# A hybrid decoder layer in one launch: the norm's feature factors move into the weights on GpSimd, x tiles and gate rows are made further ahead, and the running maxima take one scan

## What is computed

```python
xn = x * rsqrt(mean(x*x, -1) + 1e-6) * norm_gain          # rows factor, then features factor
proj = xn @ w_in                                          # 1024 -> 9*512 + 8
gb, gc, hc, zc, q, k, v, o, zm, ig, fg = split(proj)
y_conv = gb * short_conv(gc * hc) * silu(zc)
lf = log_sigmoid(fg + b_fgate); ig = ig + b_igate         # 4 heads, per token
b = cumsum(lf)                                            # within chunks of 128
m_t = max(b + m_prev, max_{s<=t}(b_t - b_s + ig_s))       # running maximum, carried over chunks
h, c, n, m = mlstm_chunk(q, k, v, ig, lf, c, n, m)        # 4 heads of 128, chunk after chunk
y_m = rms(h) * mh_norm_gain * sigmoid(o) * silu(zm)
y = rmsnorm(x + concat(y_conv, y_m) @ w_out, final_norm_gain)
```

## Time and profile before

| | us |
|---|---|
| median of 3 runs (lowest, highest) | 1136.21 (1135.74, 1137.62) |
| the profiled execution, its own time | 1135.65 |
| its span, first to last instruction | 1133.9 |
| PE busy in the span | 1071.8 (95%) |
| DVE busy | 526.0 (46%) |
| ACT busy | 338.8 (30%) |
| POOL busy | 258.3 (23%) |
| mean granted TensorE clock | 0.983 |

### The profile page before, as it was taken

The page is one execution under the profiler, slowest core; times in us unless marked ns, Lnnn a source line. Parts: engine busy times, 40 slices in busy tenths (PEclk is TensorE's granted clock), DMA queues, the critical chain, the costliest instruction groups (busy, mean ns, idle before and its releaser), DMA issues. The chain is left out here.

```text
span 1133.9 us, 17984 instructions
## 1 busy us (share of the span) xinstructions
PE 1071.8 (95%) x7186; PEld 607.4 (54%) x7186; DVE 526.0 (46%) x1018; ACT 338.8 (30%) x672; POOL 258.3 (23%) x332
## 2 busy tenths in 40 slices
PE   1789989989999999999999999999999999999996
PEld 1646545445566655556566556465656565444442
DVE  5667765655533443445443433544433323334333
ACT  5453333424321323243223232432222222221111
POOL 6101220302020223120213131211121111442322
PEclk9879999999999999999999999999999999999998
DMA  9453150415220031172101213510212053255652
GB/s 268 94 140 72 49 131 24 102 43 159 63 85 7 12 93 61 41 206 81 48 8 49 74 44 112 171 36 20 83 47 89 19 165 142 88 192 209 236 208 84
DMA packets 124311, 109.25 MB, mean 96 GB/s; under 512 B 42392, under 2 KB 109092, under 8 KB 124228
## 3 DMA queue, kind: packets, MB, share of 16 engines
q1 hardware_dynamic: 84160, 66.78, 20.3%
q0 software_dynamic: 7600, 25.03, 6.2%
q10 hardware_dynamic: 32468, 16.30, 5.2%
HBM read 65.95 MB, written 33.41 MB: 88 GB/s over the span
## 5 line engine op out<-in xcount | busy, mean ns | idle before, releaser
L783 PE MATMUL bank<-xTh,Wh 128*128 128x512 f16 (+2 forms) x1304 | 423.3, 344 | 3.7 <-DMA xTl<-to 2.3
L784 PE MATMUL bank<-xTl,Wh 128*128 128x512 f16 (+2 forms) x1304 | 425.9, 343 | 0.0
L785 PE MATMUL bank<-xTh,Wl 128*128 128x512 f16 (+2 forms) x1304 | 425.4, 343 | 0.0
L785 PEld LDWEIGHTS bank<-xTh,Wl 128*128 128x128 f16 x1304 | 129.8, 100 | 121.2 <-issue 2.2
L783 PEld LDWEIGHTS bank<-xTh,Wh 128*128 128x128 f16 x1304 | 129.7, 100 | 112.4 <-DMA xTl<-to 2.5
L784 PEld LDWEIGHTS bank<-xTl,Wh 128*128 128x128 f16 x1304 | 129.8, 100 | 109.4 <-issue 3.5
L792 PE MATMUL bank<-Wh,xTh 128*128 128x128 f16 x544 | 94.4, 221 | 3.9 <-DVE ysum L160 3.9
L793 PE MATMUL bank<-Wl,xTh 128*128 128x128 f16 x544 | 94.3, 221 | 0.0
L794 PE MATMUL bank<-Wh,xTl 128*128 128x128 f16 x544 | 94.3, 221 | 0.0
L160 DVE SCALAR_TENSOR_TENSOR Wl<-wst,Wh 128x1024 f16<-128x1024 f32 x36 | 46.5, 1291 | 32.8 <-ACT Wh L160 30.9
L160 ACT ACTIVATE tz<-bank 128x512 f32<-128x512 f32 x32 | 19.1, 597 | 136.5 <-PE bank L785 135.7
(11 more groups left out here) (328 smaller groups left out, 1542.0 us busy)
## 6 DMA issues: line engine op xcount, KB each, us to landing
wst<-in_w_in ACTq DMA_DIRECT2D x27, 512.0 KB, 4.2
xs<-in_x_prompt SPq DMA_DIRECT2D x26, 512.0 KB, 4.2
y_ops<-ysumst POOLq DMA_DIRECT2D x16, 512.0 KB, 3.2
w_ops<-xs SPq DMA_DIRECT2D x16, 448.0 KB, 4.1
out<-xs POOLq DMA_DIRECT2D x11, 512.0 KB, 2.9
Wh<-y_ops SPq DMA_DIRECT2D x12, 448.0 KB, 3.4
Wl<-y_ops SPq DMA_DIRECT2D x12, 448.0 KB, 4.1
wst<-in_w_in SPq DMA_DIRECT2D x9, 512.0 KB, 5.6
```

What stands on the lines that cost most here:

```text
L783: mm(out, wh[:, k, :], xh, start=(k == 0), stop=False)
L784: mm(out, wh[:, k, :], xl, start=False, stop=False)
L785: last = mm(out, wl[:, k, :], xh, start=False, stop=(k == KT - 1))
```

## The change

Four things change.

1. The feature factors `norm_gain` no longer multiply x. They are loaded as 8 rows beside the other small parameters, transposed with them into `par`, and POOL multiplies each staged weight tile by them in place (`gain_w`, [128, 8 x 128] f32 by a [128, 8] broadcast), 36 times, and the gate weights once. ACT's `split_w` waits for POOL (w_gained) where it waited for the load. `x_gain` is gone (17 DVE passes); the row factor goes into `x_high_part` as ACT's scale and into `x_low_part` as DVE's scalar. The 512 KB broadcast load of the factors is gone.
2. The x units are made ahead by a table for each block (X_SQUARE, X_PARTS), with a third alternating buffer in the place of the factors; SP issues the turns of units 0 to 4 together, and the loads that stood between them behind.
3. The gates pass of units 1 to 4 stands ahead of the last quarter of the first K tile; the later passes at the end of HC in blocks 1 and 2 (before: ZC), the scans at the half of ZC (before: O) and the rows at the half of O. The mixed tokens' gate rows have buffers of their own.
4. The four maxima scans of a block are one scan over 512 tokens with a row `carry` added, which holds b of the chunk's end at each chunk's start.

```diff
-X_SQUARE = {K: 0, Q: 1, GC: 2, HC: 3}
-X_GAIN = {K: 0, Q: 1, GC: 2, HC: 3}
-X_PARTS = {V: 0, GC: 1, HC: 2, GB: 3}
+X_SQUARE = [{Q: 6, GC: 7, HC: 8, ZC: 9, O: 10}, {K: 11, V: 12, GC: 13, HC: 14}, {K: 15, V: 16}]
+X_PARTS = [{Q: 5, GC: 6, HC: 7, GB: 8, O: 9, ZM: 10}, {V: 11, Q: 12, HC: 13, GB: 14}, {V: 15, Q: 16}]
+GATES_AT = [ZC, HC, HC]
+SCAN_AT = [O, ZC, ZC]
+TURN_AT = [ZM, O, O]
...
+            def gain_w(g, t):
+                pool.wait_ge(w_in_s[t % STAGES], g * (16 * NT // STAGES) + 16 * (t // STAGES + 1))
+                w = wst[t % STAGES]
+                pool.tensor_tensor(w[:, :, :], w[:, :, :], gain.unsqueeze(2).broadcast_to([P, KT, P]), ALU.mult).then_inc(w_gained, 1)
...
+            x_power(4)
+            gain_w(0, 1)
+            gain_w(0, 2)
...
+            x_power(5)
+            gain_w(0, 3)
+            gain_w(0, 4)
+            gain_w(0, 5)
+            for unit in range(6, 9):
+                x_power(unit)
+                gain_w(0, unit)
...
-            def pool_block(g, b, first):
+            def pool_block(g, b, first, following):
+                def weights(*tiles):
+                    for t in tiles if following == "weights" else ():
+                        gain_w(g + 1, t)
+                weights(K, V)
                 if not (first and b == 0):
                     store_y(g if b else g - 1, b - 1 if b else NB - 1, 1)
                     y_operands(g if b else g - 1, b - 1 if b else NB - 1)
+                weights(Q)
                 if not (first and b == 0):
                     store_sums(g if b else g - 1, b - 1 if b else NB - 1)
+                weights(GC, HC, GB)
...
                 store_y(g, b, 0)
+                weights(ZC, O)
...
                 pool.tensor_tensor(hrs[:, :], hms[:, :], halves[:, :], ALU.pow).then_inc(h_rs, 1)
+                weights(ZM)
...
                     elif first and b == 0 and t == K:
                         for c in range(CH):
+                            if c == CH - 1:
+                                pe.wait_ge(states_in, 16 * 2)
+                                use_t1(2)
+                                nc.tensor.transpose(T1[:, 0:STATES_IN], ...).then_inc(t1_full, 1)
+                                gates(x_units(0), MIX, BT, 3)
                             x_turned(pe, 1 + c)
...
             def split_w(g, t):
-                act.wait_ge(w_in_s[t % STAGES], g * (16 * NT // STAGES) + 16 * (t // STAGES + 1))
+                act.wait_ge(w_gained, g * NT + (t + 1))
...
-                act.wait_ge(x_gained, unit + 1)
-                mark(fn(x_high_rows(unit)[0:n, :], x_raw[i][0:n, :], ACT.Copy).then_inc(x_high, 1), x_high, unit + 1)
+                act.wait_ge(x_rs, unit + 1)
+                mark(fn(x_high_rows(unit)[0:n, :], x_raw[i][0:n, :], ACT.Copy, scale=rsx[0:n, unit:unit + 1]).then_inc(x_high, 1), x_high, unit + 1)
...
-                for c in range(CH if unit else 1):
-                    before, length = CH * (unit - 1) + c + 1 if unit else 0, P if unit else META
-                    sl = slice(c * P, c * P + length)
-                    did(scan(mrow[:, sl], a[:, sl], a[:, sl], mst[:, before:before + 1], ALU.max, ALU.max))
-                    end = c * P + length - 1
-                    did(tt(mst[:, before + 1:before + 2], bcum[:, end:end + 1], mrow[:, end:end + 1], ALU.add))
+                    did(copy(chunks(carry)[:, 1:CH, 0], ends[:, 0:CH - 1]))
+                    did(scan(mrow[:, :], carry, a, mst[:, first_chunk:first_chunk + 1], ALU.add, ALU.max))
+                    did(tt(mst[:, first_chunk + 1:first_chunk + 1 + CH], ends, chunks(mrow[:, :])[:, :, P - 1], ALU.add))
```

More of the change, by code:

```diff
@@ L103, in t1_uses @@
         names += [("state", t - V)] if b == 1 and t in (V, Q, GC) else []
-        names += {ZC: ["gates"], ZM: ["next cols"] if b == NB - 2 else []}.get(t, []) if first else []
+        names += ["gates"] if first and t == GATES_AT[b] else []
+        names += ["next cols"] if first and b == NB - 2 and t == ZM else []
     return names
@@ L365, in x_units, with gate_rows @@
             return range(1 + CH * b, 1 + CH * (b + 1))
+        def gate_rows(unit, n):
+            rows_ = (ehm[0:GR, :], zsm[0:H, :], Gm[0:H, :]) if unit == 0 else (grow, gt, lf)
+            return [x[:, 0:n] for x in rows_]
         def x_turned(eng, unit):
@@ L604, in _ @@
             step(pool.memset(mst[:, :], 0.0))
-            for tile, first_of, rest, start in ((restart, chunks(restart[:, :]), 1.0, 0.0), (remix, samples(remix), 1.0, 0.0),
+            step(pool.memset(rows[0:32, :], 0.0))
+            step(pool.memset(rows[32:GR, :], 1.0))
+            x_power(3)
+            for tile, first_of, rest, start in ((restart, chunks(restart), 1.0, 0.0), (remix, samples(remix), 1.0, 0.0),
                                                (forget, forget[:, :].rearrange("p (b t) -> p b t", t=DS), 0.0, NEG)):
@@ L688, in pool_block @@
                     y_operands(g if b else g - 1, b - 1 if b else NB - 1)
-                if first:
-                    for c in range(1, CH):
-                        x_power(1 + CH * (b + 1) + c)
+                weights(Q)
+                for unit in ((), (13,), ())[b] if first else ():
+                    x_power(unit)
                 if not (first and b == 0):
                     store_sums(g if b else g - 1, b - 1 if b else NB - 1)
+                for unit in ((), (14,), ())[b] if first else ():
+                    x_power(unit)
+                weights(GC, HC, GB)
                 if b == 0:
@@ L696, in pool_block @@
                     pool.tensor_tensor(hm[:, 4:5], hm[:, 3:4], halves[0:MIX, 0:1], ALU.pow).then_inc(mx_rs, 1)
+                if first and b == 0:
+                    x_power(9)
+                if b == 0:
                     store_mixed(g, 0)
@@ L874, in at_end @@
                 n = nth(g, b)
-                if first and b == 0 and t == K:
-                    gates(x_units(0), MIX, BT, 3)
                 if t == Q:
@@ L909, in at_end @@
                        start=True, stop=True).then_inc(t1_full, 1)
-                if first and t == ZC:
+                if first and t == GATES_AT[b]:
                     gates(x_units(b + 1), tok0(b + 1), BT, t1(g, b, "gates", first))
@@ L1161, in at_half @@
             def at_half(g, b, t, first):
-                if first and b == 0:
-                    for tile in SPLIT_AT_HALF.get(t, ()):
-                        split_w(0, tile)
                 if t == V and not (first and b == 0):
@@ L1421, in gate_turn @@
             def gate_turn(unit, tok, n):
-                t = gt[:, 0:n]
+                t = gate_rows(unit, n)[1]
                 a = t if unit else rows[0:H, :]
@@ L1552, in at_half @@
                     update(g, b, 0)
+                if first and b == 0:
+                    for tile in SPLIT_AT_HALF.get(t, ()):
+                        split_w(0, tile)
                 if t == O:
```

201 lines of the change are left out of this document (101 added, 100 removed).

## The result

| | before | after |
|---|---|---|
| median, us (15 runs each) | 1136.21 (1135.39 to 1138.37) | 1140.75 (1137.65 to 1144.7) |
| the profiled execution, its span | 1135.65, 1133.9 | 1141.33, 1139.5 |
| PE, DVE, ACT, POOL busy | 1071.8, 526.0, 338.8, 258.3 | 1071.2, 521.9, 340.3, 325.0 |

A forecast was written before the change was run, and what follows sets the result against it. PE was taken to bound nearly everything; 1135.65 - 26 (early) + 29.7 (late) = 1139.4, with the median 0.56 above that run 1140, rounded to 1140.5 us for stacked waits; range 1125 to 1153.

The forecast's parts named there:

- The late part: Weight blocks (block 3 of groups 0, 1 and 2): tiles delayed by POOL's multiplies cost +29.7 us, bounds +19 and +38.
- chunk step 3 behind ZC's multiply: Three weight blocks: ZC's multiply behind the conv store makes PE late by 3.2 us each, bounds 2.7 and 4.5.
- K, groups 1 and 2: K's weights in groups 1 and 2: the multiply adds its full 2.3 us to PE's wait in each.
- GC and chunk step 1: GC's late multiply delays ZC's bank and chunk step 1: 2.9 us in groups 1 and 2, 1.4 in group 0.
- half clock: Weight blocks: waits bring half-clock stretches, costing 1.7 us behind ZC in three blocks, and more behind K in two.
- The price of a multiply: POOL's in-place f32 multiply of a 128x1024 weight tile takes 2.3 us, bounds 2.13 and 2.53.
- The early part: First 265 us: earlier start, gate chain and x units, and fewer waits give -26 us, bounds -32 and -18.
- The term between: Between sel and blocks 1 and 2: half of a half-clock stretch saved, -1.7 us; shorter V wait and its clock, -3.0.
- The weight path is hidden: Rival: ACT and DVE have more in hand, late part +12 to +19, early -27, about 1126 us; chance 0.20.
- the gate chain runs clear: Rival: group 0's gate chain escapes the multiplies, columns at 46, early -32, late +29.7, 1134 us; chance 0.17.
- Stacking in full: Rival: every weight tile from Q to ZM late in all three blocks, late +38, early -22, 1152 us; chance 0.15.
- The lock takes whole instructions everywhere: Rival: each multiply also stops small DVE operations in the gate chain, columns at 53, 1143 us; chance 0.13.

The follow-up runs named there:

- no_multiply: Changed kernel without POOL's multiplies for the weights of head groups 1 to 3, so the feature factors are missing there; 1113.23 us, 0.9794 of before.
- sel_first: Changed kernel with POOL reordered, K and V weights a block earlier, group 0's tile 3 multiply in DVE's idle time, tiles 4 and 5 behind sel; 1113.41 us.
- behind_rows: Changed kernel with POOL's multiplies for tiles 3, 4 and 5 of group 0 waiting until the gate chain has its rows; 1144.38 us.
- four_scans: Changed kernel with the running maxima again made by four scans of 128 with an add each; 1149.02 us.

## Why the prediction was right

**The late part, forecast +29.7, measured +29.2.** It was the term with the widest bounds, and nearly every step holds in size (waits from PE's rows after, less the 2.2 of before; three blocks together):

| step | forecast | measured |
|---|---|---|
| chunk step 3 behind ZC's multiply | 3 x 3.2 = 9.6 | 2.63 + 3.06 + 2.63 = 8.3 |
| K, groups 1 and 2 | 2 x 2.3 = 4.6 | 2.95 + 3.66 - 2.2 = 4.4 |
| GC and chunk step 1 | 2 x 2.9 + 1.4 = 7.2 | 2.56 + 0.2 + 1.50 + 1.87 + 0.8 = 6.9 |
| half clock | 3 x 1.7 + 2 x 1.6 = 8.3 | PE's busy time for the same matmuls 504.2 - 494.6 = 9.6 |

The last line comes from the stretch between k's transposes in block 3 of group 0 and those in block 0 of group 3, before and after (columns as in the earlier trace rows):

```profile
268.49:765.32 496.83, 494.63 (x3538) 289.90 (x3537) 219.94 (x443) 152.87 (x312) 110.29 (x128) 1.00 0.24 73
244.89:770.96 526.07, 504.21 (x3539) 292.24 (x3538) 230.80 (x443) 152.89 (x312) 157.62 (x152) 0.98 0.23 69
```

The clock came out near in sum and wrong in place, as these PE stretches after show (us, busy, clock, DMA share, GB/s):

```profile
281.23:285.00 3.77, 3.77 (x20) 1.00 0.00 0
494.47:497.79 3.32, 3.32 (x8) 0.50 0.63 161
512.17:518.26 6.09, 6.09 (x17) 0.50 0.00 0
706.68:709.41 2.73, 2.73 (x9) 0.50 0.21 57
746.96:750.37 3.41, 3.41 (x12) 0.50 0.02 5
```

PE is busy for 15.6 us at half clock in them, which costs 7.8; the other 1.8 of the 9.6 I can't place. My rule, that a wait over 2 us brings a stretch of half clock, failed: none stands behind the wait of 2.63 at 281 or that of 2.95 at 472, 6.1 us of it behind that of 3.06 at 512, and 3.3 us behind the wait on u at 494, where I had priced none. That the sum fits is partly luck.

So is the term for K. no_multiply has 3.2 us of waits there without any multiply, so the multiplies add 3.4 us and not 4.6, and the new schedule adds 1.0 that I had at nothing.

**The price of a multiply, forecast 2.3 with bounds 2.13 and 2.53, was wrong**: 1887 ns undisturbed, below my lower bound. I carried the step between two f32 operations of 256 and 512 elements on, and took the lower bound from one with an f16 input. The estimate of 2.25 that I had made from the figure in GPSIMD Engine Reference of the Trainium skill, "Elementwise — side-by-side cycle accounting", is about as far off. At ZC the sum didn't suffer: what the multiply saved (0.4) the wait for POOL took (Wl takes 1.77 instead of 1.23).

**The early part, forecast -26, measured -23.6.** The gates pass ended at 33.8 (forecast 32.5), the columns started at 52.45 (51, bounds 46 to 53) behind a wait of 6.58 (4 to 8), and the product with `sel` stood at 58.80 (58). Blocks 1 and 2 gave 12.1 (12.4), with waits of 1.67 and 1.65 at chunk steps (1.6). The term between, "-1.7" and "-3.0" for the clock and V of block 1, came to 3.2 instead of 4.7. From the product with `sel` to k's transposes of block 1, before and after:

```profile
67.13:137.64 70.51, 68.49 (x516) 41.65 (x517) 49.23 (x99) 28.44 (x53) 10.24 (x16) 0.93 0.32 76
58.80:126.12 67.32, 63.81 (x518) 38.56 (x516) 50.08 (x94) 35.21 (x63) 19.41 (x24) 1.00 0.54 122
```

The clock gave 4.7 us, more than the 3.4 that I had put on it: no half clock is left there. But PE's waits grew by 1.5 instead of shrinking by 1.3. The one at V shrank from 2.02 to 1.37 only, and two are new, 0.94 for the mixed tokens' `dpm` and 1.19 at the columns of block 1.

**The rivals.** "The weight path is hidden" and "the gate chain runs clear" fall by the rows above. "Stacking in full" falls by group 0, where PE waited only 0.79 and 2.63. "The lock takes whole instructions everywhere", to which I gave 0.13, is true as a mechanism: a 4x3 copy took 1.75 us beside a multiply and 0.16 without. As the Trainium skill has it (SBUF — State Buffer, "Who interferes with whom"), a DVE instruction with two SBUF inputs contends with a GpSimd instruction that reads SBUF, and so can a copy, in a mode that uses both ports; the trace agrees. The same section exempts a DVE instruction with at most one SBUF input outside the two-port modes, and sel_first agrees. There the product `kw` reads a bank and keeps its 0.69 beside POOL's multiply, and `eh` with both inputs in SBUF takes 2.04 instead of 0.69:

```profile
52.71 1.90 POOL L612 TENSOR_TENSOR wst<-wst,par 128x1024 f32<-128x1024 f32 x1 [12.12 <-DVE sel L163]
52.73 0.69 DVE L163 TENSOR_TENSOR kw<-bank,sel 128x512 f32<-128x512 f32 x1
...
56.34 1.90 POOL L612 TENSOR_TENSOR wst<-wst,par 128x1024 f32<-128x1024 f32 x1
56.75 2.04 DVE L163 TENSOR_TENSOR eh<-eh,qf 128x512 f32<-128x512 f32 x1 [1.06 <-ACT eh L163]
```

That rival was nearer with the place (52.45 for its 53, my 51). But behind_rows, without multiplies in the chain, has the columns at 48.13 and not at 46, so part of the 52.45 is a chain that is longer than I counted. The rival's time, 1143, lies 2.5 above my forecast and doesn't decide between us: the measured 1140.75 came with an early part that gave 2.4 us less than forecast and a late part that cost 0.5 less.

## What to carry to other kernels

Work put on an idle engine is paid by where it stands in the queues of that engine and of those behind it. With 27 multiplies of 1.9 us the weight blocks took 29.2 us more than before in one order and 1.3 in another. When a change moves the time little, compare milestones of both traces before averages; here -24 and +29 hid in +0.4%, and the loss could be taken out without touching the gain. Moving an operation off a critical chain helps only if its consumers have that time in hand as well (behind_rows, sel_first).

## What the runs showed of the hardware

- POOL holds DVE even for tiny operations: a 128x2 copy took 1.83 us beside a multiply and 0.17 without, a 4x3 copy 1.75 (0.16), an 80x2 operation 1.85 (0.17). POOL is slowed too: the multiply that began at 41.25, while DVE's scan ran, took 2.55 us instead of 1.90.
- POOL's f32 multiply of 1024 elements with a broadcast factor takes 1.89 us where nothing holds it, its subtraction of the same size with an f16 input 2.13.
- A microsecond more of waiting can bring stretches of half clock that cost more than it. In four_scans three such stretches (118, 166 and 227 us) stand behind waits of 2.06, 2.74 and 2.71 where the changed kernel waited 1.37, 1.67 and 1.65 and has none, and the one around the columns lasts 10.24 us instead of 6.83. The length of the wait doesn't settle it alone: behind the same wait of 2.63 at chunk step 3 of group 0 four_scans has a stretch and the changed kernel none.
